# Squares of a pair of rotary tiles added on GpSimd before TensorE sums them

## The reference, cut to what matters

```python
def _rmsnorm(x, w):
    x32 = x.astype(jnp.float32)
    y = x32 * lax.rsqrt(jnp.mean(x32 * x32, axis=-1, keepdims=True) + EPS)
    return (y * w.astype(jnp.float32)).astype(x.dtype)
...
    q = _axial_rope(_rmsnorm(q, q_norm_w), row, col)
    k = _axial_rope(_rmsnorm(k, k_norm_w), row, col)
```

## Time and profile before

| what | value |
|---|---|
| median of 3 runs | 4435.95 us (4435.03 to 4436.82) |
| the profiled execution, own time | 4429.47 us |
| its span, first to last instruction | 4427.6 us |
| mean granted TensorE clock | 0.946 of 2.4 GHz |
| busy PE / PEld | 3932.4 / 3072.8 us |
| busy DVE / ACT / POOL | 2696.4 / 1855.9 / 670.3 us |
| small matmuls L369, in both layers | 896 rows |
| GpSimd squares L411 | 28, of 3.60 us |

### The profile page before, as it was taken

How to read it: one execution, slowest core, us unless ns; L and a number is a source line. 1 busy time by engine, 2 the same in 40 slices (tenths; PEclk the granted TensorE clock), 3 DMA queues, 4 the chain that set the end, 5 groups by cost and what they waited for, 6 DMA issues and landing times. The chain is left out here.

```text
span 4427.6 us, 57501 instructions
## 1 busy us (share of the span) xinstructions
PE 3932.4 (89%) x19701; PEld 3072.8 (69%) x19701; DVE 2696.4 (61%) x3334; ACT 1855.9 (42%) x2590; POOL 670.3 (15%) x760
## 2 busy tenths in 40 slices
PE   3999997789799999987979999966997999999693
PEld 2788885589766666656758888845995666666483
DVE  5453044567688888874255411735777888888432
ACT  3221111245377777761132211122554777777310
POOL 0011100596400000000000110036941000000000
PEclk9999998899899999998989999987998999999896
DMA  6111154645510000026231212644453000000635
GB/s 248 65 63 65 66 175 164 152 117 143 142 38 23 21 23 24 23 69 191 109 128 62 71 58 91 242 124 121 130 159 90 21 24 24 23 20 17 174 147 204
DMA packets 338791, 426.21 MB, mean 96 GB/s; under 512 B 106440, under 2 KB 256120, under 8 KB 315840
## 3 DMA queue, kind: packets, MB, share of 16 engines
q1 hardware_dynamic: 335744, 403.10, 29.6%
q10 hardware_dynamic: 2880, 20.97, 1.2%
HBM read 276.04 MB, written 147.94 MB: 96 GB/s over the span
## 5 line engine op out<-in xcount | busy, mean ns | idle before, releaser
L1744 DVE TENSOR_REDUCE att_sb_part<-att_banks 128x1 f32<-128x512 f32 x992 | 658.7, 685 | 150.6 <-PE att_banks L1629 144.9
L1732 ACT ACTIVATE att_sb_probs<-att_banks 128x1024 f32<-128x1024 f32 x512 | 524.9, 1025 | 379.0 <-PE att_banks L1655 378.8
L1762 DVE TENSOR_TENSOR att_sb_p_lo<-att_sb_probs,att_sb_p_hi 128x1024 fp32r<-128x1024 f32 x512 | 623.4, 1218 | 20.6 <-ACT att_sb_p_hi L1736 18.4
L1736 ACT ACTIVATE att_sb_p_hi<-att_sb_probs 128x1024 fp32r<-128x1024 f32 x512 | 543.2, 1061 | 16.2
L358 PE MATMUL proj_banks<-proj_sb_h_hi,proj_sb_w_hi 128*128 128x512 f32 x1600 | 519.5, 406 | 6.2 <-DVE proj_sb_w_lo L493 6.2
L358 PE MATMUL proj_banks<-proj_sb_h_lo,proj_sb_w_hi 128*128 128x512 f32 x1600 | 516.7, 404 | 0.0
L358 PE MATMUL proj_banks<-proj_sb_h_hi,proj_sb_w_lo 128*128 128x512 f32 x1600 | 516.6, 404 | 0.0
L1053 PE MATMUL dn_banks<-dn_sb_room 128*128 128x128 f32 x3072 | 379.4, 284 | 55.0 <-DMA dn_sb_room<-proj 21.6
L1053 PEld LDWEIGHTS dn_banks<-dn_sb_room 128*128 128x128 f32 x3072 | 367.9, 198 | 76.7 <-DMA dn_sb_room<-proj 30.1
L1671 PE MATMUL att_banks<-att_sb_p_hi,att_sb_v_hi 128*65 128x512 f32 x1024 | 406.9, 397 | 12.4 <-DVE att_sb_o L1768 11.0
L1654 PE MATMUL att_banks<-att_sb_q,att_sb_k 128*128 128x512 f32 x1024 | 413.1, 403 | 1.9 <-DVE att_sb_q L1756 1.9
(11 more groups left out here) (226 smaller groups left out, 5632.4 us busy)
## 6 DMA issues: line engine op xcount, KB each, us to landing
proj<-proj_sb_out SPq DMA_DIRECT2D x40, 1024.0 KB, 4.6
dn_sb_kq<-proj SPq DMA_DIRECT2D x64, 512.0 KB, 5.3
proj_sb_w_raw<-in_w_in SPq DMA_DIRECT2D x52, 516.0 KB, 5.2
dn_sb_room<-proj SPq DMA_DIRECT2D x32, 768.0 KB, 5.3
att_sb_q<-att_q SPq DMA_DIRECT2D x64, 256.0 KB, 2.9
out_sb_x<-x_res SPq DMA_DIRECT2D x16, 1024.0 KB, 6.5
x_res<-out_sb_x SPq DMA_DIRECT2D x16, 1024.0 KB, 4.2
proj_sb_pad<-proj SPq DMA_DIRECT2D x24, 512.0 KB, 5.3
```

The lines of the kernel that those rows point to most:

```text
L1732: nc.scalar.activation(probs[:, pair % 2], ps[:, 2 * (pair % 2):2 * (pair % 2) + 2, :], ACT.Exp, scale=SCALE).then_inc(s["exp_done"], 1)
L1736: nc.scalar.activation(p_hi[:, pair % SLOTS], probs[:, pair % 2], ACT.Copy).then_inc(s["hi_done"], 1)
L1744: nc.vector.tensor_reduce(part[:, w // NQ, w % NQ:w % NQ + 1], ps[:, 4 + w % 2, :], AX.X, ALU.max) \
L1762: nc.vector.tensor_tensor(p_lo[:, pair % SLOTS], probs[:, pair % 2], p_hi[:, pair % SLOTS].bitcast(F32), ALU.subtract).then_inc(s["lo_done ...
```

## The change

For the six rotary tiles GpSimd now squares the pair's first tile into `small` (a 128 x 2048 buffer that is otherwise not used until the sums are done), the second tile into `sq`, and adds the first into `sq`. TensorE sums only the added squares, in `pair_sum`: 16 sums for a pair instead of 32. Those of pair 12/13 lie in the second half of tile 15, those of 14/15 in that of tile 17, and those of 16/17 in the second half of tile 18. The squares of the DeltaNet tiles stay as they were. DVE no longer copies and adds sums; ACT reads the pairs' sums from PSUM.

```diff
-STATS = T_Z - T_Q
+STATS = T_AQ - T_Q + (T_Z - T_AQ) // 2
...
-        first_sums = stats(0, PAIR_TILES * NC * 4).rearrange("p (m c r) -> p m c r", m=PAIR_TILES, r=4)
+        first_squares = small[:]
...
+                def pair_sum(i, n):
+                    pair = i - T_AQ // 2
+                    if n == 0:
+                        pe.wait_ge(s["pair_squared"], pair + 1)
+                    col = (pair + T_AQ - T_Q) * 4 * NC + 4 * n
+                    mm = nc.tensor.matmul(sums[:, bass.ds(col, 4)], sq[:, n * P:(n + 1) * P], c.quarters[:],
+                                          start=True, stop=True)
+                    if n == NC - 1:
+                        mm.then_inc(s["stats_done"], 1)
...
-                with pe.Fori(T_Q // 2 + 1, T_Z // 2) as i:
+                with pe.Fori(T_Q // 2 + 1, T_AQ // 2 + 1) as i:
                     for u in range(2):
                         tile_half(i, u, 0)
 
                         tile_half(i, u, 1, [[lambda n=n: square_sum(i - 1, u, n)] for n in range(NC)])
+                with pe.Fori(T_AQ // 2 + 1, T_Z // 2) as i:
+                    tile_half(i, 0, 0)
+                    tile_half(i, 0, 1)
+                    tile_half(i, 1, 0)
+                    tile_half(i, 1, 1, [[lambda n=n: pair_sum(i - 1, n)] for n in range(NC)])
                 i = T_Z // 2
-                tile_half(i, 0, 0, [[lambda n=n: square_sum(i - 1, 0, n)] for n in range(NC)])
-                late = [[]] * 12 + [[lambda n=n: square_sum(i - 1, 1, n)] for n in range(8)]
-                late += [[lambda n=n: square_sum(i - 1, 1, n), lambda n=n: square_sum(i - 1, 1, n + 1)] for n in range(8, NC, 2)]
+                tile_half(i, 0, 0)
+                late = [[]] * 12 + [[lambda n=n: pair_sum(i - 1, n)] for n in range(8)]
+                late += [[lambda n=n: pair_sum(i - 1, n), lambda n=n: pair_sum(i - 1, n + 1)] for n in range(8, NC, 2)]
...
-                with pool.Fori(T_Q // 2, T_Z // 2) as i:
+                with pool.Fori(T_Q // 2, T_AQ // 2) as i:
...
+                with pool.Fori(T_AQ // 2, T_Z // 2) as i:
+                    t = i * 2
+                    pool.wait_ge(s["out_ready"], t + 2)
+                    pool.wait_ge(s["pair_squared"], i - T_AQ // 2)
+                    nc.gpsimd.tensor_tensor(first_squares, out[:, 0, :], out[:, 0, :], ALU.mult).then_inc(s["squared"], 1)
+                    pool.wait_ge(s["out_ready"], t + 3)
+                    pool.wait_ge(s["stats_done"], T_AQ - T_Q + i - T_AQ // 2)
+                    nc.gpsimd.tensor_tensor(sq[:], out[:, 1, :], out[:, 1, :], ALU.mult).then_inc(s["squared"], 1)
+                    pool.wait_ge(s["squared"], t + 4)
+                    nc.gpsimd.tensor_tensor(sq[:], sq[:], first_squares, ALU.add).then_inc(s["pair_squared"], 1)
...
-                act.wait_ge(s["summed"], 2)
-                nc.scalar.activation(rms.rearrange("p m r c -> p m c r"), first_sums, ACT.Sqrt, bias=c.eps[:, 0:1],
+                act.wait_ge(s["stats_done"], STATS)
+                pair_sums = sums[:, (T_AQ - T_Q) * 4 * NC:STATS * 4 * NC].rearrange("p (m c r) -> p m c r", m=PAIR_TILES, r=4)
+                nc.scalar.activation(rms.rearrange("p m r c -> p m c r"), pair_sums, ACT.Sqrt, bias=c.eps[:, 0:1],
...
-                    nc.vector.tensor_copy(first_sums, att_sums[:, :, 0]).then_inc(s["summed"], 1)
-                    dve.wait_ge(s["summed"], 1)
-                    nc.vector.tensor_tensor(first_sums, att_sums[:, :, 1], first_sums, ALU.add).then_inc(s["summed"], 1)
```

More of the change, by code:

```diff
@@ L189, in input_projection @@
              "conv_step taps_kept conv_done out_ready out_stored0 out_stored1 ba_hi ba_split ba_stored edges "
-             "squared stats_done summed root inv_rms turned rows_copied rows_stored qk_w_loaded rope_loaded "
+             "squared pair_squared stats_done root inv_rms turned rows_copied rows_stored qk_w_loaded rope_loaded "
              "ab_loaded0 ab_loaded1 inv_loaded0 inv_loaded1 products added scaled hi lo rope_stored0 rope_stored1")
@@ L541, in inverse_rms @@
                 def inverse_rms():
-                    att_sums = sums[:, (T_AQ - T_Q) * 4 * NC:STATS * 4 * NC] \
-                        .rearrange("p (m f c r) -> p m f c r", m=PAIR_TILES, f=2, r=4)
                     dve.wait_ge(s["stats_done"], STATS)
-                    nc.vector.tensor_copy(first_sums, att_sums[:, :, 0]).then_inc(s["summed"], 1)
-                    dve.wait_ge(s["summed"], 1)
-                    nc.vector.tensor_tensor(first_sums, att_sums[:, :, 1], first_sums, ALU.add).then_inc(s["summed"], 1)
                     nc.vector.tensor_reduce(c.sums[:].rearrange("p t c -> p (t c)"),
```

## The result

The changed kernel took 4403.1 us (median of 4 runs, 4399.7 to 4406.9) beside 4435.9 for the kernel before: ratio 0.9926, 95% interval 0.9909 to 0.9943. The forecast was 4415.3 with a range of 4412 to 4420, so the direction was right and the size was not: 32.7 us were gained where 20.6 were forecast. The profiled execution of the changed kernel has a span of 4405.1 us against 4427.6, which is 22.5 less.

What follows compares the result with a forecast made beforehand. PE was taken to bound the input projection; 96 removed sums at 0.2148 us gave −20.6 us, all other parts 0, so the median would go from 4435.95 to 4415.3 us, range 4412 to 4420.

Steps and rivals of the forecast that it cites:

- The price of a sum: Input projection on PE: 0.2148 us for each small sum matmul, 96 removed in both layers, −20.6 us.
- Short tiles of 22.49 us: Tiles 14 and 16 lose all their sums and should take 22.49 us, as a gate tile does.
- the hidden root: After the sums: two small DVE operations go, with 6.6 us of cover before PE needs the reciprocal; cost 0, gain 0.
- no step at the new loop: One more loop on TensorE and one on GpSimd: taken as 0, bounded by an issue wait of 3.5 us.
- a free sum: Rival: in the projection a sum was nearly free and removing it brings nothing; 4435.6 us, chance 2%.
- a late chain: Rival: GpSimd's square and add come late for PE in tile 18, kernel slower, 4442 us; chance 1%.
- an end held by something beside the gate tiles: Rival: rotary work of DVE and SP, not PE, sets the projection's end; half the gain, 4425.6 us; chance 3%.
- three signs of being wrong: PE waits on the added squares, short tiles take more than 22.5 us, or PE stops entering the new loop.
- I take 3.8: GpSimd's add of two buffers: 3.79 us by the median of a half-length operation, 6.64 by its longest; hidden.
- 8.0 us to spare: Tile 18: copy, handoff, square and add take 8.7 us of the 16.7 before PE's first late sum.
- Up to about 8 us: DVE's weight splits beside GpSimd: some 2.7 us longer each, up to about 8 beside square and add; cost 0.
- the spread: High and low ends: 2 us below and 1 us above for run spread; code after the projection stable to about 1 us.

Runs made afterwards that it cites:

- the four gains with and without fillers: Changed kernel against before, with no, 8, 24 or 48 idle small matmuls a layer in tile 19's second half: 25.4, 12.0, 10.9, 23.0 us gained.
- d_adds_only: Kernel before plus an unused GpSimd add of 128x2048 behind each rotary pair's second square, all sums kept: 4435.6 us, ratio 1.0002.

## Why the prediction failed

*Right.* The price of a sum (0.2148 us) and their number: 10.31 us in each layer between the copies, for 10.3 forecast. Short tiles of 22.49 us, no wait of PE for GpSimd or for a split, the hidden root, no step at the new loop. The rivals of a free sum, of a late chain and of an end held by something beside the gate tiles are refuted by the same rows. None of the three signs of being wrong appeared.

*Mis-sized, without effect.* "I take 3.8" for the add, by L1276's 1.896 us at half the length: measured 5.46, within the 6.64 held as bound. Of the 8.0 us to spare 6.3 were left. L1276 is not "the trace's other two-input operation on GpSimd": L1302 reads two buffers of 128 x 512 in 1.416 us on the average, L1308 in 1.270, and four times these, 5.7 and 5.1, lie on both sides of 5.46. Both inputs of L1276 are broadcast views. "Up to about 8 us" for a split beside square and add: measured 3.5. The first score matmul came at 1210.27 us, not at 1209.0.

*The step that failed* is the spread: "2 us for the spread of the runs (4435.03 to 4436.82) and of what follows", and "such a stretch is stable to about 1 us", from two layers of one execution. Executions of the kernel before differ by up to 22 us (4424.4 to 4446.9 in 73 runs on three chips, up to 21 on one), the first output projection took 215.6 to 228.7 us over the 14 profiled ones, and averages of programs stray from their work by up to 11 us. The 32.7 us are: 20.6 for the sums; 3.7 because before's four runs (4435.9) lie above its average of 73 (4432.1); 2.9 because the changed kernel's four lie below its average of 9 (4406.0); and 5.5 (within 3 of error) between the averages. The last part mixes chips; on chip 12 alone it is 4.8. Its cause is open. It is no gain of the change's own that another program keeps: of the four gains with and without fillers (25.4, 12.0, 10.9 and 23.0) two lie below 20.6. The forecast's own profiled execution, 6.5 us under the median, was a sign of that spread that I had noted and not used. By the averages the change is worth 25 to 26 us between these two programs, and 20.6 of it are the change's own. That the first result lay another 6.6 us beyond was the luck of four runs on either side.

## What to carry to other kernels

Price a small matmul in a stream of big ones by the distance between starts: a float32 one with 128 stationary and 4 moving columns cost 0.214 us here, so add on an idle engine first, or store its operands as fp32r and pay about half. A few runs that agree within 2 us don't bound the spread of a kernel with waits and bulk loads in it. The change's own gain is told from the program's luck by the stretch that it touches, from one engine's instruction to another's with no wait between, and by a control that refills what was removed.

## What the runs showed of the hardware

GpSimd's `tensor_tensor` over 128 x 2048 float32 took 3.60 us with one buffer as both inputs, multiply or add, and 5.46 with two. The Trainium skill ("GPSIMD Engine Reference", section "Elementwise — side-by-side cycle accounting") gives 4.497 us for an add; no run here shows it.

DVE's split with two SBUF inputs, 1.23 us alone, ended 1.1 us after the end of the GpSimd operation it had met (so 3.3 to 3.5 us, 3.96 in the earlier trace rows, and 1.71 in d_adds_only, where it met the end of an add). It was not held through the add that followed the square. GpSimd's own times did not change.

The 0.111 and 0.214 us of a sum agree with the Trainium skill's weight load of 128 columns ("TensorE: Matmul & The Clock Gate", section "LDWEIGHTS (loading the stationary operand)"), 107 ns by its formula, once and twice.

After the same wait of 3.1 us in layer 2, TensorE's granted clock was 0.50 for some 5.9 us in the execution of the kernel before and 1.00 at once in that of the changed one.
